# Half-array matmuls of a two-block transformer kernel rewritten for the whole 128x128 array

## Chip, cores and metric

The kernel runs on one core of a Trainium2 chip (trn2). The metric is device time in microseconds for one execution.

## What is computed

Two blocks of two layers each, in float32, on one sequence of 512 tokens of width 1024. A layer of the first block is a mixer (gated delta rule, top-k sparse attention and a gated linear recurrence side by side) and a feed-forward part; a layer of the second block is feed-forward, mixer (a linear recurrence, stick-breaking attention and forgetting attention), feed-forward. The parts that the change touches, cut to the core:

```python
# gated delta rule: 4 heads of 128, chunks of 64 tokens
T  = triangular_solve(eye + M, eye)                 # M strictly lower triangular, 64 x 64 for each chunk
u0 = T @ (beta * v);  wk = T @ (beta * exp(G) * k)
def step(state, ...):                               # 8 chunks, one after the other
    u = u0_c - w_c @ state
    o = qd_c @ state + qk_c @ u
    state = state * gl_c + kd_c.T @ u
# sparse attention, 4 heads of 64: an index score selects keys for each block of 128 queries
score = sum_h(relu(qi_h @ ki.T) * wi_h)
o = softmax(q_h @ k_sel.T / 8) @ v_sel
# second block, 4 heads of 64 each
z = q @ k.T / 8;  y_sb  = weights(z) @ v            # stick-breaking
y_fox = softmax(q @ k.T / 8 + Fq - Fk) @ v          # forgetting
```

## The kernel before

Activations lie transposed: features on the partitions, the 512 tokens along the free axis. Every large product (projections, feed-forward, output) is made in three passes of rounded operands: high part by high part, low by high, high by low (`hh,wh`, `hl,wh`, `hh,wl` in the profile; `wh` and `wl` are made from each loaded weight chunk `raw` by one ScalarE and one VectorE instruction). These are called dense here. Such a matmul is one record in the trace; the small products inside the mixers are plain float32 and leave two records each. All matmuls go through one helper line, L175 (transposes L181), all activations through L190, tensor-tensor operations of VectorE and GpSimd through L193, so that groups are told apart by the tile names.

The program is not issued in the order of its text. Each logical strand (a lane: `dn_prepare0`, `dn_scan1`, `dsa_choose`, `dsa0`, `hg1`, `fox0`, `sb0`, `weights`, `dense` ...) only records its steps with what they wait for. `interleave` then ranks the steps by their longest remaining path, plus hand-set leads for single lanes (`LEADS`, `WAYS`), and `schedule` writes a fixed instruction order for each engine by a cost model. On TensorE it knows the tile form of each matmul (`tile_of`: 128 or 64 rows, 128, 64 or 32 columns), counts a drain of the array when the form changes, keeps a model of the array's clock, prefers dense work when the clock would otherwise fall, and may put in empty matmuls (`nothing`, L259, `spinner,zeros`). Waits between engines stay semaphore waits.

The four mixers are the places where small products stand. `mixer1` runs twice, `mixer2` twice:

- `gates` turns the rows of wi, beta and the decay (4 transposes from partitions 64 to 127 of `tmp`).
- `dn_project`, `dn_prepare(p)` for two pairs of heads: the triangle of each 64-token chunk is inverted by doubling, in 5 rounds of 64x64 products (`bA`, `bB`, `bC`, `bMT`; two chunks at a time, one on partitions 0 to 63, one on 64 to 127). The solved triangle `Z` (`bB`) then multiplies `bV` (giving `u0`, tile `du`) and `bK` (giving `wk`, tile `dwk`), one 64-token chunk at a time.
- `dn_scan(r)`: eight steps for each pair; a step takes `wk` by the state (`ds,dwk`), subtracts it from `u0` into `u` (`du`), makes the new state from `kdec` and `u` (`du,dkd`), and the output from state by q (`dq,ds`) and `u` by `qk` (`dqk,du`).
- `dsa_choose`: index scores (`ki,qi`), then 16 rounds of max and match_replace on VectorE. `dsa_project` writes queries, keys and values over the same tiles `qi` and `ki`; `dsa_attend` runs 16 steps (4 query blocks, 4 heads), each with a score product (`ki,qi`), softmax, transposes, and the product with the values (`apt,av`), all through the one bank B[6].
- the gated linear recurrence (`hg_tile`): 64x64 products throughout (`hq,hk`, `ht`, `mod_sum`, `ha,hi`).
- `mixer2`: `sb_attention` (`sbq,sbk` scores, `sw,sbv` values), `fox_attention` (`fxk,fxq` scores, `fpt,fxv` values), `lru`. The values of two heads fill the two partition halves of one bank `bo`, which ScalarE copies out once for each pair of heads.

A head of 64 occupies 64 partitions, so the score products load 64 rows of the array, the value products write 64 columns, and the scan does either. The program's `project` hands out the dense projections, 28 tiles in `mixer1`, and the strands use up this dense work while they run.

## Time and profile before

| | |
|---|---|
| median of 3 runs | 3846.35 us (3844.14 to 3847.4) |
| profiled execution, its own time | 3846.75 us |
| its span | 3845.0 us |
| TensorE busy | 3753.6 us, 98% |
| VectorE, ScalarE, GpSimd busy | 2025.5, 1590.1, 184.1 us |
| mean granted TensorE clock | 0.961 |

The granted clock is given as a share of 2.4 GHz: 1.00 is that level and 0.50 is 1.2 GHz, and a value between is a stretch that had both. A busy TensorE is not TensorE at its peak: ends of matmuls are modelled in the record, so that a matmul that drains or that runs at half clock also counts as busy. How fast the array is fed is seen better in the times at which weight loads (PEld) start. "mean ns" of a matmul holds its latency, not only its share of the stream.

### The profile page before, as it was taken

How to read it: one execution, taken by the hardware profiler on the slowest of the kernel's cores; microseconds unless marked ns; L12 is line 12 of the kernel's file. 1: busy time of each engine (PE TensorE's matmuls, PEld its weight loads, DVE VectorE, ACT ScalarE, POOL GpSimd, SP SyncE). 2: the span in 40 equal slices, each digit the busy share in tenths (PEclk: the TensorE clock that was granted, in tenths of full speed). 3: DMA queues.
4: the chain of work that ended last, by engine and by line, in shares of the span. 5: the costliest groups of instructions: out<-in, count | busy, mean ns of one | idle time of the engine just before them, and what ended most of it. 6: DMA issues, size and time to landing. Idle time of an engine off the chain costs nothing.

```text
span 3845.0 us, 50935 instructions
## 1 busy us (share of the span) xinstructions
PE 3753.6 (98%) x21067; PEld 3062.8 (80%) x21067; DVE 2025.5 (53%) x3365; ACT 1590.1 (41%) x2465; POOL 184.1 (5%) x256
## 2 busy tenths in 40 slices
PE   9999999999999999999999998999999999989999
PEld 7877788887767688888888865988888888668888
DVE  6955377647764367745444465544443335554332
ACT  7445543326353343323222478322232225863221
POOL 1010100002010010001000010000000001000000
PEclk9978899999997799999999998999999999999999
DMA  3101134442111034443444311244422332112232
GB/s 118 62 28 34 55 116 145 146 143 81 56 45 34 1 110 148 145 153 109 148 148 149 104 50 44 92 150 147 151 98 98 96 96 69 50 39 89 98 98 89
DMA packets 108694, 368.27 MB, mean 96 GB/s; under 512 B 14128, under 2 KB 16560, under 8 KB 108464
## 3 DMA queue, kind: packets, MB, share of 16 engines
q1 hardware_dynamic: 108464, 365.02, 28.8%
q8 instruction: 167, 2.74, 0.3%
q14 instruction: 63, 0.52, 0.0%
HBM read 360.78 MB, written 4.19 MB: 95 GB/s over the span
## 4 chain that ended last, share of the span: by engine, by line
PE 78%; ACT 6%; DVE 4%; issue 2%; POOL 1%; POOLq 0%; ACTq 0%; DVEq 0%
PE bank L175 77%; ACT L398 2%; PE bank L259 1%; ACT tmp L190 1%; ACT wh L190 1%; DVE tmp L196 1%; PE bank L181 0%; DVE wl L193 0%; DVE score L217 0%; ACT lr L190 0%; DVE ast L214 0%; ACT hh L190 0%; POOL x L193 0%; ACT fl L190 0%; ACT lu L190 0%
## 5 line engine op out<-in xcount | busy, mean ns | idle before, releaser
L175 PE MATMUL bank<-hh,wh 128*128 128x512 f32 (+2 forms) x3424 | 1290.5, 377 | 15.8 <-ACT lg L190 10.4
L175 PE MATMUL bank<-hl,wh 128*128 128x512 f32 (+2 forms) x3424 | 1289.0, 376 | 0.0
L175 PE MATMUL bank<-hh,wl 128*128 128x512 f32 (+2 forms) x3424 | 1285.8, 376 | 0.1
L190 ACT ACTIVATE wh<-raw 128x1024 fp32r<-128x1024 f32 (+1 forms) x542 | 559.1, 1036 | 1464.2 <-PE bank L175 1457.5
L193 DVE TENSOR_TENSOR wl<-raw,wh 128x1024 fp32r<-128x1024 f32 (+1 forms) x542 | 652.5, 1207 | 809.9 <-ACT wh L190 809.4
L175 PEld LDWEIGHTS bank<-hh,wh 128*128 128x128 f32 (+1 forms) x3424 | 651.6, 190 | 144.4 <-issue 33.7
L175 PEld LDWEIGHTS bank<-hl,wh 128*128 128x128 f32 (+1 forms) x3424 | 651.6, 190 | 116.4 <-issue 12.3
L175 PEld LDWEIGHTS bank<-hh,wl 128*128 128x128 f32 (+1 forms) x3424 | 652.1, 190 | 115.6 <-issue 9.1
L175 PE MATMUL bank<-ah,wh 128*128 128x512 f32 (+1 forms) x1188 | 437.4, 368 | 0.0
L175 PE MATMUL bank<-ah,wl 128*128 128x512 f32 (+1 forms) x1188 | 436.9, 368 | 0.0
L175 PE MATMUL bank<-al,wh 128*128 128x512 f32 (+1 forms) x1188 | 436.5, 367 | 0.0
L175 PEld LDWEIGHTS bank<-ah,wh 128*128 128x128 f32 x1188 | 224.6, 189 | 35.8
L175 PEld LDWEIGHTS bank<-ah,wl 128*128 128x128 f32 x1188 | 224.6, 189 | 35.6
L175 PEld LDWEIGHTS bank<-al,wh 128*128 128x128 f32 x1188 | 224.6, 189 | 35.2
L398 ACT ACT_TABLE_LOAD x190 | 243.8, 1283 | 3.4
L196 DVE SCALAR_TENSOR_TENSOR mod_sum<-raw,cact,mod_sum 128x512 f32<-128x512 f32 x252 | 189.1, 750 | 29.3 <-DMA raw<-in_ada_dram 25.2
L193 DVE TENSOR_TENSOR gv<-bank,gv 128x512 f32<-128x512 f32 x88 | 60.9, 692 | 214.6 <-PE bank L175 213.0
L196 DVE SCALAR_TENSOR_TENSOR gv<-bank,small,gv 128x511 f32<-128x511 f32 (+1 forms) x176 | 130.9, 746 | 2.5
L190 ACT ACTIVATE ah<-gv 128x512 fp32r<-128x512 f32 x132 | 81.9, 620 | 104.0 <-DVE gv L193 104.0
L193 DVE TENSOR_TENSOR al<-gv,ah 128x512 fp32r<-128x512 f32 x132 | 90.7, 687 | 21.1 <-ACT ah L190 20.8
L196 DVE SCALAR_TENSOR_TENSOR x<-bank,dmod,x 128x512 f32<-128x512 f32 (+1 forms) x58 | 37.7, 658 | 120.3 <-PE bank L175 120.2
L193 POOL TENSOR_TENSOR x<-x,tmp 128x256 f32<-128x256 f32 x56 | 44.9, 827 | 855.7 <-DVE tmp L196 855.7
(367 smaller groups left out, 3772.3 us busy)
## 6 DMA issues: line engine op xcount, KB each, us to landing
raw<-in_up_dram SPq DMA_DIRECT2D x264, 512.0 KB, 3.3
raw<-in_ada_dram SPq DMA_DIRECT2D x144, 512.0 KB, 4.2
raw<-in_in_dram SPq DMA_DIRECT2D x88, 512.0 KB, 3.3
raw<-in_down_dram SPq DMA_DIRECT2D x96, 448.0 KB, 3.3
raw<-in_down_dram SPq DMA_DIRECT2D x48, 512.0 KB, 3.5
raw<-in_out_dram SPq DMA_DIRECT2D x32, 512.0 KB, 3.3
x<-in_x_dram SPq DMA_DIRECT2D x16, 256.0 KB, 5.0
raw<-in_in2v_dram SPq DMA_DIRECT2D x8, 512.0 KB, 3.7
```

Of the source, the lines that this page charges most:

```text
L175: s = self.put(lambda e: e.matmul(out, lhsT, rhs, **kw), records * max(records * n, 2 * m) / 2.4)
L190: return self.put(lambda e: e.activation(out, x, func, **kw), cost, tables)
L193: return self.vector(lambda e: e.tensor_tensor(out, a, b, op), width(out))
L196: return self.vector(lambda e: e.scalar_tensor_tensor(out, a, scalar, b, op0, op1), width(out), 125.0)
L259: s = Step(Queue(self, "nothing", "pe"), lambda e: e.matmul(out[:, 0:n], zeros, rhs, start=alone, stop=alone), [], n / 2.4)
L398: engine.preload_act_table_set(s.load)
```

## The change

Every product listed above that used half of the array's rows or columns is rewritten so that it addresses all 128 rows and 128 columns.

- Scan: `u` keeps zeros in the partitions of the other chunk (both `u` buffers of each pair are cleared once at the start of the mixer, and each buffer serves chunks of one half only). `kdec`, `qk` and `wk` are then taken over all 128 partitions or all 128 columns of the pair of chunks.
- Solved triangles: a new tile `bZ`, over the places of `bM` and `bMT`, is cleared by GpSimd after the last use of `bMT`; two ScalarE copies (64 partitions by 8x64) lay the two triangles of a pair of chunks on its diagonal. One matmul then serves both chunks, for `u0` and for `wk`. `bM` and `bMT` come free only after these products.
- Scores: `qi`, and in `mixer2` `sk` and `fq`, get a slot for each head, with zeros in the other head's partitions; so the copy out of PSUM is two instructions of 64 partitions in place of one of 128. The tiles are cleared by GpSimd at the start of the mixer.
- Values: the stationary operand is a 128-column pair of value blocks, the result is taken from the half that belongs to the head. In `mixer2` the bank `bo` is copied out once for each head (64 partitions by 512) and the next head's values wait for that.
- `gates` and `dsa_project` copy and transpose 128 rows in place of 64.
- `ysa`, `ysb` and `yfx` move into the slots of used queries or keys; the copies that write them wait for the score products that read them.

`LEADS` and `WAYS` stay as they are; the fixed order on each engine is worked out anew by `schedule`. The products of `hg_tile`, the five rounds of `dn_prepare` and its `chunks` and turn of `bM` keep their forms. The diff, cut to its core:

```diff
+    mem.bZ = mem.place("bZ", [P, 8, P], F32, b_at + 2048 * 3)
...
+    mem.av = mem.place("av", [P, 5, 64], F32, at)
+    at += 1024
...
-    mem.qi, mem.ki = put("qi", [P, 2, S]), put("ki", [P, S])
-    mem.av = put("av", [P, 4, 64])
+    mem.qi, mem.ki = put("qi", [P, 4, S]), put("ki", [P, S])
+    mem.ysa = mem.qi.rearrange("p (t x) s -> p t x s", x=2)[:, :, 0, :]
...
+    mem.padded = []
+    q = mem.lane("padding")
+    q.pool.wait_ge(before)
+    mem.padded.append(q.pool.memset(mem.qi[:, :, :], 0.0).then_inc(q.pool.sem, 1))
+    for v in mem.pairs:
+        for u in v.u.slots:
+            q.pool.wait_ge(before)
+            u.free = [q.pool.memset(u.ap[:, :, :], 0.0).then_inc(q.pool.sem, 1)]
...
-        rows = q.dve.tensor_copy(t.ap[64:128, :], b.ap[64:128, :]).then_inc(q.dve.sem, 1)
+        rows = q.dve.tensor_copy(t.ap[:, :], b.ap[:, :]).then_inc(q.dve.sem, 1)
         b.free = [k1, k2, rows]
         b = B[2]
-        for j in range(4):
-            q.pe.wait_ge(rows, b.free)
-            turned = q.pe.transpose(b.ap[:, 64 * j:64 * j + 64], t.ap[64:128, P * j:P * j + P], mem.k("ident")[64:128, 64:128]).then_inc(q.pe.sem, 1)
+        turned = transposes(mem, q, b, [t.ap[:, P * j:P * j + P] for j in range(4)], rows)
...
-        bMT.free, X.free, Y.free = [mx], [mx], [yz]
+        X.free, Y.free, apart = [mx], [yz], []
+        q.pool.wait_ge(mx, bM.free)
+        blank = q.pool.memset(mem.bZ[:, :, :], 0.0).then_inc(q.pool.sem, 1)
+        for h in range(2):
+            r0 = slice(64 * h, 64 * h + 64)
+            q.act.wait_ge(zs, blank)
+            apart.append(q.act.activation(mem.bZ[r0, :, 64 * h:64 * h + 64], Z.ap[r0, :, :], ACT.Copy).then_inc(q.act.sem, 1))
...
-                for h in range(2):
-                    r0 = slice(64 * h, 64 * h + 64)
-                    q.pe.wait_ge(zs, bv[e], b.free)
-                    m = q.pe.matmul(b.ap[r0, P * j:P * j + P], Z.ap[r0, 2 * j + e, :], bV.ap[r0, e, j, :], start=True, stop=True).then_inc(q.pe.sem, 1)
+                q.pe.wait_ge(apart, bv[e], b.free)
+                m = q.pe.matmul(b.ap[:, P * j:P * j + P], mem.bZ[:, 2 * j + e, :], bV.ap[:, e, j, :], start=True, stop=True).then_inc(q.pe.sem, 1)
...
-            b, m2 = prep.next(), None
-            for h in range(2):
-                r0 = slice(64 * h, 64 * h + 64)
-                other = m2
-                for j in range(4):
-                    at = P * j + 64 * h
-                    q.pe.wait_ge(zs, bk[e], other, b.free)
-                    m2 = q.pe.matmul(b.ap[:, at:at + 64], bK.ap[r0, e, j, :], Z.ap[r0, 2 * j + e, :], start=True, stop=True).then_inc(q.pe.sem, 1)
+            b = prep.next()
+            for j in range(4):
+                q.pe.wait_ge(apart, bk[e], b.free)
+                m2 = q.pe.matmul(b.ap[:, P * j:P * j + P], bK.ap[:, e, j, :], mem.bZ[:, 2 * j + e, :], start=True, stop=True).then_inc(q.pe.sem, 1)
...
-        bV.free, bK.free, Z.free = [m], [m2], [m2]
+        Z.free = apart
+        bM.free = bMT.free = [m, m2]
+        bV.free, bK.free = [m], [m2]
...
-                    m = q.pe.matmul(b.ap[r0, P * e:P * e + P], v.wk[:, e, at:at + 64], state.ap[:, e, :], start=True, stop=True).then_inc(q.pe.sem, 1)
+                    m = q.pe.matmul(b.ap[:, P * e:P * e + P], v.wk[:, e, P * j:P * j + P], state.ap[:, e, :], start=True, stop=True).then_inc(q.pe.sem, 1)
...
-                    m = q.pe.matmul(b.ap[:, P * e:P * e + P], v.kdec[r0, e, j, :], u.ap[r0, e, :], start=True, stop=True).then_inc(q.pe.sem, 1)
+                    m = q.pe.matmul(b.ap[:, P * e:P * e + P], v.kdec[:, e, j, :], u.ap[:, e, :], start=True, stop=True).then_inc(q.pe.sem, 1)
...
-                mo = q.pe.matmul(o, u.ap[r0, e, :], v.qk[r0, 2 * j + e, :], start=n == 0, stop=True).then_inc(q.pe.sem, 1)
+                mo = q.pe.matmul(o, u.ap[:, e, :], v.qk[:, 2 * j + e, :], start=n == 0, stop=True).then_inc(q.pe.sem, 1)
...
+    def heads(q, i, b, done, free, scale=None):
+
+        ready = []
+        for x in range(2):
+            rows = slice(64 * x, 64 * x + 64)
+            q.act.wait_ge(done, free)
+            ready.append(q.act.activation(mem.qi[rows, 2 * i + x, :], b.ap[rows, :], ACT.Copy, scale=scale).then_inc(q.act.sem, 1))
+        return ready
...
-                m = q.pe.matmul(b.ap[:, 0:n], mem.qi[lo:lo + 64, h // 2, P * i:P * i + P], mem.ki[lo:lo + 64, 0:n], start=True, stop=True).then_inc(q.pe.sem, 1)
+                b, t = dsa.next(), logit.next()
+                q.pe.wait_ge(qi_ready[h], gt["ki"], b.free)
+                m = q.pe.matmul(b.ap[:, 0:n], mem.qi[:, h, P * i:P * i + P], mem.ki[:, 0:n], start=True, stop=True).then_inc(q.pe.sem, 1)
...
+                at = 64 * ((k - h % 2) % 4)
                 q.pe.wait_ge(s, v_ready, b.free)
-                m = q.pe.matmul(b.ap[lo:lo + 64, 0:P], mem.av[:, k, :], pt.ap[:, P * k:P * k + P], start=k == 0, stop=k == i).then_inc(q.pe.sem, 1)
+                m = q.pe.matmul(b.ap[:, 0:P], pairs[:, at:at + P], pt.ap[:, P * k:P * k + P], start=k == 0, stop=k == i).then_inc(q.pe.sem, 1)
...
-            q.act.wait_ge(m)
+            q.act.wait_ge(m, multiplied[i, h], multiplied[i, h - h % 2])
...
-    mem.sq, mem.sk = put("sbq", [P, 2, S]), put("sbk", [P, 2, S])
+    mem.sq, mem.sk = put("sbq", [P, 2, S]), put("sbk", [P, 4, S])
...
+    for y in (mem.sk, mem.fq):
+        q.pool.wait_ge(before)
+        mem.padded.append(q.pool.memset(y[:, :, :], 0.0).then_inc(q.pool.sem, 1))
...
+            b, done = project(10 + i)
+            d[1, i] = []
+            for x in range(2):
+                rows = slice(64 * x, 64 * x + 64)
+                q.act.wait_ge(done, mem.padded)
+                d[1, i].append(q.act.activation(mem.sk[rows, 2 * i + x, :], b.ap[rows, :], ACT.Copy).then_inc(q.act.sem, 1))
+            b.free = d[1, i]
...
+                    for x in range(2):
+                        rows = slice(64 * x, 64 * x + 64)
+                        q.dve.wait_ge(r_ready, g8, mem.padded)
+                        d[n, i].append(q.dve.scalar_tensor_tensor(mem.fq[rows, 2 * i + x, :], b.ap[rows, :], mem.g8[rows, 0:1], r.ap[rows, :], ALU.mult, ALU.mult).then_inc(q.dve.sem, 1))
...
-            m = q.pe.matmul(b.ap[:, 0:n], mem.fq[lo:lo + 64, ti, P * i:P * i + P], mem.fk[lo:lo + 64, ti, 0:n], start=True, stop=True).then_inc(q.pe.sem, 1)
+            m = q.pe.matmul(b.ap[:, 0:n], mem.fq[:, h, P * i:P * i + P], mem.fk[:, ti, 0:n], start=True, stop=True).then_inc(q.pe.sem, 1)
+            multiplied.append(m)
...
-            if not (hp or i):
-                sums[:] = [bo.free]
             for k in range(i + 1):
-                q.pe.wait_ge(s, v_ready[k], sums)
-                m = q.pe.matmul(bo.ap[lo:lo + 64, P * i:P * i + P], mem.fv[:, k, 64 * h:64 * h + 64], pt.ap[:, P * k:P * k + P], start=k == 0, stop=k == i).then_inc(q.pe.sem, 1)
+                q.pe.wait_ge(s, v_ready[k], bo.free)
+                m = q.pe.matmul(bo.ap[:, P * i:P * i + P], mem.fv[:, k, P * ti:P * ti + P], pt.ap[:, P * k:P * k + P], start=k == 0, stop=k == i).then_inc(q.pe.sem, 1)
...
+            if i == 3:
                 q = mem.lane("fox0")
-                q.act.wait_ge(sums, columns, rows)
-                done.append(q.act.activation(mem.yfx[:, ti, :], bo.ap[:, :], ACT.Copy).then_inc(q.act.sem, 1))
+                q.act.wait_ge(sums, multiplied)
+                done.append(q.act.activation(mem.yfx[lo:lo + 64, ti, :], bo.ap[lo:lo + 64, :], ACT.Copy).then_inc(q.act.sem, 1))
...
-                    m = q.pe.matmul(z, mem.sk[lo:lo + 64, ti, P * i:P * i + P], mem.sq[lo:lo + 64, ti, P * i:S], start=True, stop=True).then_inc(q.pe.sem, 1)
+                    m = q.pe.matmul(z, mem.sk[:, h, P * i:P * i + P], mem.sq[:, ti, P * i:S], start=True, stop=True).then_inc(q.pe.sem, 1)
...
-                    q.pe.wait_ge(w_ready[i], v_ready[i], sums)
-                    m = q.pe.matmul(bo.ap[lo:lo + 64, P * i:S], mem.sv[:, i, 64 * h:64 * h + 64], w.ap[:, a0:a0 + n], start=i == 0, stop=i == 3).then_inc(q.pe.sem, 1)
+                    q.pe.wait_ge(w_ready[i], v_ready[i], bo.free)
+                    m = q.pe.matmul(bo.ap[:, P * i:S], mem.sv[:, i, P * ti:P * ti + P], w.ap[:, a0:a0 + n], start=i == 0, stop=i == 3).then_inc(q.pe.sem, 1)
...
-                sums.append(m)
-            q.act.wait_ge(sums, columns, rows)
-            done.append(q.act.activation(mem.ysb[:, ti, :], bo.ap[:, :], ACT.Copy).then_inc(q.act.sem, 1))
-            bo.free = [done[-1]]
-        return done
+                q.act.wait_ge(m, multiplied)
+                done.append(q.act.activation(mem.ysb[lo:lo + 64, ti, :], bo.ap[lo:lo + 64, :], ACT.Copy).then_inc(q.act.sem, 1))
```

## Rows read from the trace of the kernel before

**Rows 1.** The page: busy time and share of TensorE; granted clock in 40 slices.

```profile
PE 3753.6 (98%) x21067; PEld 3062.8 (80%) x21067; DVE 2025.5 (53%) x3365; ACT 1590.1 (41%) x2465; POOL 184.1 (5%) x256
...
PEclk9978899999997799999999998999999999999999
```

**Rows 2.** Windows of the four mixers: busy us of each engine, granted clock, DMA share, GB/s.

```profile
84.00:444.00 360.00, 345.58 (x2982) 270.71 (x2981) 227.73 (x473) 177.11 (x276) 39.31 (x44) 0.87 0.12 39
950.00:1340.00 390.00, 371.99 (x2957) 275.87 (x2955) 214.91 (x444) 164.53 (x264) 39.92 (x41) 0.84 0.11 35
2190.00:2406.00 216.00, 199.29 (x926) 139.16 (x925) 120.53 (x209) 164.02 (x263) 16.92 (x34) 0.94 0.15 49
3215.00:3440.00 225.00, 203.18 (x966) 141.46 (x965) 119.50 (x210) 165.56 (x267) 18.80 (x35) 0.96 0.15 49
```

**Rows 3.** Timeline of the weight loads over the four mixers: first row, last row.

```profile
84.00 0.41 PEld L259 LDWEIGHTS bank<-spinner,zeros 128*128 128x128 f32 x2
...
3439.88 0.19 PEld L175 LDWEIGHTS bank<-hh,wh 128*128 128x128 f32 x1
```

**Rows 4.** Timeline of weight loads: start, length, rows*columns of the array, count.

```profile
326.10 0.30 PEld L175 LDWEIGHTS bank<-dq,ds 128*128 128x128 f32 x2
326.31 0.19 PEld L175 LDWEIGHTS bank<-hh,wl 128*128 128x128 f32 x1
...
1221.78 0.19 PEld L175 LDWEIGHTS bank<-hl,wh 128*128 128x128 f32 x1
1222.01 0.19 PEld L175 LDWEIGHTS bank<-hh,wl 128*128 128x128 f32 x1
1222.55 0.19 PEld L175 LDWEIGHTS bank<-apt,av 128*64 128x64 f32 x2 [0.35 <-issue]
1222.91 0.19 PEld L175 LDWEIGHTS bank<-hh,wh 128*128 128x128 f32 x1 [0.17 <-issue]
```

**Rows 5.** The same timeline where the clock is at half.

```profile
295.65 0.50 PEld L175 LDWEIGHTS bank<-dq,ds 128*128 128x128 f32 x2
296.03 0.33 PEld L175 LDWEIGHTS bank<-hh,wl 128*128 128x128 f32 x1
...
1281.01 0.50 PEld L175 LDWEIGHTS bank<-dq,ds 128*128 128x128 f32 x2
1281.63 0.50 PEld L175 LDWEIGHTS bank<-dqk,du 64*128 64x128 f32 x2
```

**Rows 6.** The same timeline: solved triangle by bK, and by bV.

```profile
200.54 0.96 PEld L175 LDWEIGHTS bank<-bB,bK 64*128 64x128 f32 x8 [0.17 <-issue]
...
1012.90 0.85 PEld L175 LDWEIGHTS bank<-bV,bB 64*64 64x64 f32 x16 [0.17 <-issue]
```

**Rows 7.** The same timeline: two half-array products side by side.

```profile
1190.63 0.18 PEld L175 LDWEIGHTS bank<-bB,bK 64*128 64x128 f32 x1
1190.63 0.18 PEld L175 LDWEIGHTS bank<-dqk,du 64*128 64x128 f32 x1
```

**Rows 8.** Windows inside the mixers, columns as in rows 2.

```profile
252.00:300.00 48.00, 48.00 (x623) 41.16 (x623) 17.56 (x45) 7.77 (x20) 1.25 (x4) 0.50 0.01 1
312.00:372.00 60.00, 59.34 (x478) 45.16 (x476) 32.16 (x76) 40.80 (x67) 2.54 (x2) 1.00 0.11 36
1052.00:1124.00 72.00, 68.17 (x705) 52.10 (x705) 52.20 (x98) 44.24 (x71) 17.69 (x15) 1.00 0.14 45
1232.00:1310.00 78.00, 76.06 (x399) 51.18 (x400) 38.89 (x86) 34.27 (x67) 3.80 (x3) 0.56 0.06 21
372.00:408.00 36.00, 32.97 (x215) 22.28 (x216) 18.73 (x36) 19.13 (x36) 3.80 (x3) 0.72 0.09 30
2284.00:2368.00 84.00, 70.92 (x282) 47.18 (x281) 47.07 (x78) 81.40 (x110) 2.06 (x7) 0.93 0.14 45
```

**Rows 9.** Groups of instructions by form: ScalarE copy of a whole bank; GpSimd clearing.

```profile
L190 ACT ACTIVATE ysb<-bank 128x512 f32<-128x512 f32 x4 | 2.4, 594 | 7.3 <-PE bank L175 7.3
L223 POOL MEMSET wr<- 128x512 f32 x2 | 1.1, 528 | 1186.9 <-DVE x L196 1186.9
```

89 lines of the change are left out of this document (45 added, 44 removed).

## Prediction

> **What bounds the kernel now.** I read the page first. TensorE is busy for 98% of the span, and in its clock row only a few of the 40 slices stand below 9 tenths [rows 1]. They lie in the mixers, so the second view is the windows of the four mixers [rows 2], 1191 us in all. TensorE lacks 14.4, 18.0, 16.7 and 21.8 us of busy time there; VectorE and ScalarE have about half of the first two windows and ScalarE has 164 of 216 and 166 of 225 us in the last two. So `mixer1` is bound by TensorE's stream nearly throughout. `mixer2` is bound by it in its first third, and then by ScalarE, which has 81.4 of 84 us between 2284 and 2368 [rows 8]. Outside the mixers nothing that the change touches is issued.
>
> Busy says little about what TensorE does with its time, so the third view is the timeline of weight loads, from the first row to the last over the four windows [rows 3]. Merged, these windows hold 1037, 1034, 729 and 767 groups; I went through them for places where the tile form (rows*columns) changes: 244, 329, 99 and 94, together 766. What such a place costs is seen in single rows. Dense loads follow each other by 0.23 us (1221.78 to 1222.01); before a change of form the next load comes after 0.54. A small product of two records that keeps the form takes 0.21 (326.10 to 326.31), and one before a change takes 0.36 [rows 4]. So a change costs 0.31 us behind a dense matmul and 0.15 behind a small one. At half clock a small one takes 0.38 without and 0.62 with a change [rows 5], 0.24 more; behind a dense one I scale 0.31 to 0.42, an estimate.
>
> **The changed order of forms.** I took the order as it is and read the changed products as 128*128. Then 130, 225, 14 and 12 changes of form stay, and 385 go: 77 behind dense and 227 behind small ones at full clock, 75 behind small and 6 behind dense ones at half. 77 x 0.31 + 227 x 0.15 + 75 x 0.24 + 6 x 0.42 = 23.9 + 34.1 + 18.0 + 2.5 = 78.5 us, of which 22.2, 22.5, 17.6 and 16.2 lie in the four mixers. What stays in `mixer1` are mostly the 64x64 products of `hg_tile` and of the five rounds. The order will be written anew, so the count is an estimate: the scheduler can group less or more.
>
> How much lands in the time? In `mixer1` TensorE is idle for only 4% of the windows [rows 2], but its chains through VectorE and ScalarE run close behind; I take 70% of 44.7, 31 us (bounds 30% and all). In `mixer2` a faster TensorE meets ScalarE: I take 30% of 33.8, 10 us (bounds nothing and all).
>
> **Solved triangles.** The product with `bK` has eight loads in 0.96 us with the last at 0.19, 0.11 us each [rows 6]. Its 128 records become 64: 64 x 0.11 = 7 us, on the path 5. The product with `bV` has 16 loads in 0.85 us, 0.053 each [rows 6]: the two chunks already run side by side, and eight full ones at 0.11 take 0.88, so nothing is gained there. The Trainium skill, "TensorE: Matmul & The Clock Gate", section on packing small matmuls, says that tiles on different row groups run concurrently and that a short contraction alone takes as long as a full one. By it, padding never shortens a matmul and only gives concurrency away; the trace agrees for `bV` (0.053 against 0.11), and by it alone the sum would be just the loss that follows.
>
> The same concurrency happens by chance elsewhere: `bB,bK` and `dqk,du` start together at 1190.63 [rows 7]. I count 46 such starts in the four windows; full-array products can't do this, and each costs 0.11: 5 us, on the path 4.
>
> The remaining changed products keep their count, and what they load or stream keeps them at 0.11 a record (a value product with 64 columns, `apt,av`, takes the 0.36 of two records and a change, as above). More rows or columns cost nothing by these rows, except that a first load of 128 columns in place of 64 may show by half of 0.11; about 100 such starts would be 5 us at most, and I take 0.
>
> **Clock.** Two stretches are at reduced clock and made of small products of all kinds: 1232 to 1310 at 0.56, and 372 to 408 at 0.72. They pass 399 records in 78 us and 215 in 36 (5.1 and 6.0 a us), and the stretch from 312 to 372 at full clock passes 478 in 60, 8.0 a us [rows 8]. At that pace they would save 28 and 9 us, 37 in all; that is the upper bound, since dense work also stands in the fast stretch, and the lower bound is nothing. Before the clock fell, TensorE was fed with half-array products and changes of form, and both go away. I take 15. From 252 to 300 (0.50) the 64x64 products dominate and stay, so I expect no gain.
>
> The Trainium skill, same page, Part 1, says that the clock follows how busy TensorE is, and not how much of the array a matmul fills. By it the padding itself would leave the clock where it is; that is a rival below. The trace has TensorE at 76.06 busy of 78 with the clock at 0.56, so its busy row doesn't decide it.
>
> **What is added.** A ScalarE copy of a bank takes 0.59 us [rows 9], and half the partitions save nothing, as its time goes by the free axis. In each `mixer2` there are two more for `sk`, two for `ysb`, two for `yfx`: 6 x 0.59 = 3.5 us, 7 in both, in a time where ScalarE has no room; I take 5. The next head's values wait for the copy of `bo`, with nothing behind but other lanes' products, which the order puts between; 0 to 5 us a mixer, in the range. In each `mixer1`: four more copies for `qi` (2.4 us, under ScalarE's idle half), and for each pair two copies for `bZ` in the chain from the last `zs` to `u0`, 1.2 us a pair and 4.7 in all, if nothing else fills TensorE; I take 3. What waits behind them is `wk`, `u0` and the scan's first step. GpSimd clears `bZ` in 2 x 0.53 us [rows 9] while the last `yz` product and the subtraction behind it run; were it late, up to 1 us a pair. The clearing of `qi` (2.1 us), `u`, `sk` and `fq` (4.2 us) lies under the first three projections; GpSimd has 39 of 360 us of work there [rows 2]. `fq` has two more VectorE instructions, with VectorE at 120 of 216. No DMA is added. `bM` and `bMT` come free later: the second pair's first sums would have to wait for the first pair's products, which run at 200 [rows 6], before the stretch from 252 in which the second pair's rounds stand [rows 8]; nothing. Sum of the added: 8 us.
>
> **Sum.** -31 - 10 - 5 + 4 - 15 + 8 = -49 us on the profiled execution's 3846.75 (span 3845.0, 1.75 around it): 3798. The median of the runs is 0.4 lower; I leave it at 3798.
>
> **Rivals.**
> - The clock stays as it is (the page's rule): 3798 + 15 = 3813. For it: many dense-free stretches remain. Against it: with the changes of form gone the same products stand closer together.
> - Other engines take the place: ScalarE in `mixer2` gives nothing back, in `mixer1` only 30% of 44.7 lands (the scans go back and forth between TensorE and VectorE at each step), 13 + 2 for the triangles - 8 added = 7: 3840. For it: VectorE has 228 of 360 us and ScalarE 177 [rows 2]. Against it: TensorE's idle 4%.
> - All of it lands: 78.5 + 7 + 37 = 122: 3724. For it: in `mixer1` the order can even group better than I count. Against it: ScalarE in `mixer2`.
> - Slower: the dense stock runs out earlier. The projections are what keeps the clock up between the strands; with small products faster, the same leads spend them sooner, and 312 to 372 and 1052 to 1124, now at 1.00 [rows 8], fall to half. At 5.1 against 8.0 records a us such time grows by 0.56: 132 us give +74, on 3813: 3887. It decides from 34 / 0.56 = 60 us on. For it: from 252 to 300 exactly this already happened (0.50). Against it: the scheduler holds dense work back when its clock model falls.
>
> **How the numbers follow.** Chances: the forecast 0.40, clock unmoved 0.22, other engines 0.15, all of it 0.14, slower 0.09. The range has to leave out the slower case and little else: 3725 (the bound of all gains) to 3850 (past the third case, with its lost waits of `bo`). About 0.2% (7.7 us) is what a measurement of this kernel can tell from no change. Faster by more: 0.40 + 0.22 + 0.14 and half of the third case, 0.83; within: the other half, 0.08; slower: 0.09. The forecast's own range is 3780 to 3815.
>
> **What would show it.** In the timeline of weight loads the changes of form in the four mixers fall from 766 to about 380, in `mixer2` to under 20 each; `bB,bK` disappears with 64 records in its place; the windows of `mixer1` shrink by about 20 to 30 us each and those of `mixer2` by about 5; the clock of the second `mixer1` rises above 0.84. The prediction is wrong if the count falls and the windows stay (other engines), if new half-clock stretches stand where 1.00 was (dense stock), or if ScalarE's stretch in `mixer2` grows past its 7 us.

## The result, and the profile after

The changed kernel takes 3717.28 us (median of 4 runs, 3703.77 to 3719.11) against 3846.88 for the kernel before (3844.14 to 3848.83): ratio 0.9654 (0.9636 to 0.9673), 133 us of 3847 (126 to 140). I had forecast 3798, with a range from 3725 to 3850; the time lies 8 us below the range. The profiled execution took 3718.38 us, with a mean granted clock of 0.972 (before 0.961).

The page of the kernel after, the lines that answer to [rows 1]:

```profile
PE 3634.4 (98%) x20983; PEld 3055.5 (82%) x20983; DVE 2023.8 (54%) x3369; ACT 1607.3 (43%) x2496; POOL 203.4 (5%) x274
...
PEclk9979999999979999999999998999999999989999
```

The number of matmuls is nearly unchanged, and TensorE is busy for 119 us less. Since the order is made anew, the windows of [rows 2] no longer hold the same work. I therefore cut both traces at two landmarks, from the last `gv` write of the stage before a mixer to the first `gv` write of the feed-forward part behind it. The four stages take 513.4, 669.8, 434.6 and 436.0 us before and 467.8, 602.5, 422.8 and 430.4 after: -45.6, -67.4, -11.8 and -5.7. All else together changed by +1.9. Windows of these stages, before and then after (columns as in [rows 2]):

```profile
84.00:513.00 429.00, 412.24 (x3437) 333.97 (x3436) 262.68 (x551) 208.71 (x349) 52.07 (x60) 0.87 0.13 43
744.00:1414.00 670.00, 646.35 (x4483) 509.40 (x4482) 365.37 (x734) 285.47 (x484) 72.15 (x83) 0.90 0.20 65
2034.00:2468.00 434.00, 417.29 (x2207) 332.92 (x2207) 232.82 (x411) 235.22 (x385) 18.75 (x39) 0.97 0.25 80
3065.00:3501.00 436.00, 413.15 (x2189) 327.70 (x2188) 215.36 (x383) 236.80 (x384) 20.33 (x39) 0.98 0.20 64
sum 1969.00, PE 1889.03 PEld 1503.99 DVE 1076.22 ACT 966.20 POOL 163.31; mean PE 472.26 PEld 376.00 DVE 269.06 ACT 241.55 POOL 40.83
```

```profile
84.00:468.00 384.00, 370.73 (x3362) 318.03 (x3361) 257.17 (x544) 210.84 (x353) 52.13 (x58) 0.91 0.14 48
698.00:1301.00 603.00, 584.59 (x4459) 496.61 (x4458) 364.27 (x735) 298.03 (x499) 76.26 (x90) 0.94 0.22 73
1923.00:2345.00 422.00, 408.84 (x2224) 341.05 (x2224) 232.72 (x413) 234.59 (x388) 24.66 (x41) 0.97 0.25 82
2942.00:3373.00 431.00, 405.31 (x2195) 336.53 (x2194) 217.49 (x386) 238.98 (x388) 25.83 (x41) 0.97 0.20 65
sum 1840.00, PE 1769.47 PEld 1492.23 DVE 1071.65 ACT 982.43 POOL 178.89; mean PE 442.37 PEld 373.06 DVE 267.91 ACT 245.61 POOL 44.72
```

The reader is to see two things: the gain stands in TensorE's busy column (1889.0 to 1769.5, 119.6 of 129 us), and TensorE's idle rest is nearly the same (80.0 and 70.5 us). So nothing else became the bound. Two counts go with it, taken over whole stages from the timeline of weight loads and from the granted clock. Changes of form fell from 259, 353, 101 and 96 (809) to 114, 116, 14 and 16 (260). Time at half clock fell from 297 us to 194.

The added work, from the groups by form of the kernel after, answers to [rows 9]; the two lines of the solved triangles, from the timeline of weight loads, answer to [rows 6]:

```profile
L190 ACT ACTIVATE bZ<-bB 64x512 f32<-64x512 f32 x8 | 5.0, 630 | 11.4 <-DVE bB L193 11.3
L223 POOL MEMSET bZ<- 128x1024 f32 x4 | 3.8, 954 | 16.2 <-PE bank L175 16.2
L223 POOL MEMSET sbk<- 128x2048 f32 x2 | 3.6, 1811 | 0.0
L223 POOL MEMSET qi<- 128x2048 f32 x2 | 3.6, 1808 | 9.4 <-DMA x<-in_x_dram 9.3
```

```profile
183.93 1.06 PEld L175 LDWEIGHTS bank<-bZ,bK 128*128 128x128 f32 x8
184.91 0.97 PEld L175 LDWEIGHTS bank<-bV,bZ 128*128 128x128 f32 x8
```

The copies take 0.63 us (I had 0.59), the clearing 0.95 and 1.8 us (I had 1.06 and 2.1), and a full-array record about 0.12 us: eight of them, then the next group 0.98 later.

### The profile page after: what moved, and what is told of

It is laid out like the page before. It is cut to its first block, busy times and chain, and to the rows that moved or that the text cites. A ratio compares the mean times of both kernels' runs of the same rounds, so it can differ in the third digit from the quotient of the medians.

```text
span 3716.6 us, 50808 instructions
## 1 busy us (share of the span) xinstructions
PE 3634.4 (98%) x20983; PEld 3055.5 (82%) x20983; DVE 2023.8 (54%) x3369; ACT 1607.3 (43%) x2496; POOL 203.4 (5%) x274
## 4 chain that ended last, share of the span: by engine, by line
PE 86%; ACT 7%; DVE 6%; issue 1%; POOL 1%; DMA 0%; SPq 0%; DVEq 0%; ACTq 0%; POOLq 0%
PE bank L175 84%; ACT L398 3%; ACT tmp L190 1%; PE bank L259 1%; DVE wl L193 1%; PE bank L181 1%; DVE score L217 1%; ACT wh L190 1%; DVE ast L214 1%; ACT lr L190 0%; DVE tmp L196 0%; POOL x L193 0%; DVE dk L196 0%; DVE bA L193 0%; DVE dv L196 0%
## 5 line engine op out<-in xcount | busy, mean ns | idle before, releaser
L259 PE MATMUL bank<-spinner,zeros 128*128 128x512 f32 (+3 forms) x336 | 94.5, 409 | 0.0
```

The source lines that it names most:

```text
L259: s = Step(Queue(self, "nothing", "pe"), lambda e: e.matmul(out[:, 0:n], zeros, rhs, start=alone, stop=alone), [], n / 2.4)
```

## The experiments

All ratios are against the kernel before. The stage counts are those of the one profiled execution.

### Which part carries it

**`mixer2` as before, all else changed.** The layout, copies and half-array products of `mixer2` are put back:

```diff
-    mem.sq, mem.sk = put("sbq", [P, 2, S]), put("sbk", [P, 4, S])
+    mem.sq, mem.sk = put("sbq", [P, 2, S]), put("sbk", [P, 2, S])
...
-            m = q.pe.matmul(b.ap[:, 0:n], mem.fq[:, h, P * i:P * i + P], mem.fk[:, ti, 0:n], start=True, stop=True).then_inc(q.pe.sem, 1)
+            m = q.pe.matmul(b.ap[:, 0:n], mem.fq[lo:lo + 64, ti, P * i:P * i + P], mem.fk[lo:lo + 64, ti, 0:n], start=True, stop=True).then_inc(q.pe.sem, 1)
```

> The change in mixer1 alone; mixer2 is as before. Between landmarks the two mixer2 stages gave back 11.8 and 5.7 us of the 128.6. Theory A and C alike: 3717 + 17 = 3734 (3728 to 3740). If the stages interact through the order, more than 8 us away from that.

Measured: 3724.85 us, ratio 0.9677 (0.9652 to 0.9702), 9 us slower than the changed kernel by the ratios, where 17 were expected; the difference is at the edge of the interval. The two stages take 436.5 and 435.4 us with 102 and 95 changes of form: 18.7 us longer than in the changed kernel. The whole profiled execution is 14 us longer (span 3730.8 against 3716.6), so the rest of it is 4 us shorter.

**The scan alone on half the array.** Three lines are taken back:

```diff
-                    m = q.pe.matmul(b.ap[:, P * e:P * e + P], v.wk[:, e, P * j:P * j + P], state.ap[:, e, :], start=True, stop=True).then_inc(q.pe.sem, 1)
+                    m = q.pe.matmul(b.ap[r0, P * e:P * e + P], v.wk[:, e, at:at + 64], state.ap[:, e, :], start=True, stop=True).then_inc(q.pe.sem, 1)
...
-                mo = q.pe.matmul(o, u.ap[:, e, :], v.qk[:, 2 * j + e, :], start=n == 0, stop=True).then_inc(q.pe.sem, 1)
+                mo = q.pe.matmul(o, u.ap[r0, e, :], v.qk[r0, 2 * j + e, :], start=n == 0, stop=True).then_inc(q.pe.sem, 1)
```

> The changed kernel with the three products of the scan on half of the array again (352 of the records that changed in mixer1, in 3 of the 5 products of a scan step). Theory A: the scan makes most changes of form in mixer1, up to 4 for each of 32 steps; with two thirds of them back, 80 to 130 more changes, 20 to 35 us: 3737 to 3752. Theory C: the scan's rows matter for the clock between 300 and 350 and in the second layer; half-clock time up by 30 to 60 us and 15 to 40 us on the time, with few changes more. If the scan is hidden behind other work, 3717 to 3725.

Measured: 3778.91 us, ratio 0.9822 (0.9802 to 0.9842): 62 us slower than the changed kernel, with 260 more changes of form (225, 265, 14, 16). By its ratio, half of the gain hangs on the scan, and both count and time are far above what was expected (80 to 130 changes, 3737 to 3752). But the order was made anew here too: 34 of the 56 us by which the profiled execution is longer lie in the first stage, which takes 502.0 us.

### The array or the plan?

The forms of the products enter twice: on the chip, and in the cost model by which `schedule` writes the order. In the next two kernels the scheduler is told something else than what the chip does.

**Full array on the chip, planned as half.** In the changed kernel each changed product is given its old form for the planner only:

```diff
-    def matmul(self, out, lhsT, rhs, **kw):
+    def matmul(self, out, lhsT, rhs, form=None, **kw):
...
-        s.tile, s.records, s.size = tile_of(lhsT, out), records, n
+        s.tile, s.records, s.size = form or tile_of(lhsT, out), records, n
```

> The changed kernel, but the scheduler is told the old half-array forms of the changed products, so that the order is made as if nothing had been padded. Theory A (the gain is the array's: changes of form that are no longer there, both those of the old order and those that the new order can avoid): the changes of form in the four mixers come out near the 381 that the prediction counted for the old order, against 260 in the changed kernel, and at 0.2 to 0.25 us each the time is some 25 to 35 us above 3717: 3740 to 3760. Theory B (the gain is the new order's, whatever the array does): 3830 to 3850, near the kernel before. Theory C (the gain is mainly the clock, which the padded rows raise): the half-clock time in the mixers is as short as in the changed kernel (about 185 us in its four mixers, against about 280 before) and the time is 3720 to 3740 whatever the count of changes.

Measured: 3805.6 and 3805.5 us, ratio 0.9892 (0.9863 to 0.9921); two further executions took far longer (4600 us at a granted clock of 0.724, and 12442 us) and are left out, so this rests on two; why those took so long is open. This is a gain of 42 us; with the planner kept ignorant, the forecast of 49 would have come close. No theory fits: there are 428 changes of form, the time at half clock is as short as theory C wanted (184 us), and the time is 88 us above the changed kernel. Windows of its four stages:

```profile
84.00:504.00 420.00, 386.92 (x3374) 318.14 (x3373) 261.68 (x553) 210.26 (x356) 52.66 (x62) 0.93 0.13 44
734.00:1384.00 650.00, 609.06 (x4432) 500.20 (x4431) 365.71 (x735) 292.15 (x494) 74.78 (x90) 0.94 0.21 67
...
sum 1931.00, PE 1810.39 PEld 1491.29 DVE 1079.31 ACT 982.90 POOL 173.73; mean PE 452.60 PEld 372.82 DVE 269.83 ACT 245.73 POOL 43.43
```

TensorE's busy time falls by 79 us, but its idle time grows from 80 to 121. My reading, which no run tests, is that the order was laid out for slower products and the chains behind them don't keep up.

**Half array on the chip, planned as full.** The same the other way round, in the kernel before, with `form=((True, 128), (0, 0), 128, 128)` on each product that the change touches.

> The kernel before, but the scheduler is told that the changed products fill the whole array, so that it orders them as in the changed kernel, while the chip still gets half-array forms. Theory A: the real changes of form grow past the 766 of the kernel before, since nothing holds them back, and the time is 3850 to 3900. Theory B: much of the gain is there, 3740 to 3790. Theory C: the clock falls for longer than before, since the scheduler believes it high, 3860 or more.

Measured: 3797.44 us (3794.6 to 3802.3), ratio 0.9872 (0.9852 to 0.9893), with 813 changes of form on the chip; theory B had 3740 to 3790. The plan alone is worth 49 us while the array does what it did before, solved triangles included. Both kernels also shift thousands of instructions, so neither isolates the array; the next ones do.

### The array alone, in an unchanged order

These are the changed kernel with half-array operands put back but the full form told to the scheduler. The instruction order is then the same on every engine as in the changed kernel; only the extent of the operands differs. The solved triangles stay full.

```diff
+FULL = ((True, 128), (0, 0), 128, 128)
...
-                mo = q.pe.matmul(o, u.ap[:, e, :], v.qk[:, 2 * j + e, :], start=n == 0, stop=True).then_inc(q.pe.sem, 1)
+                mo = q.pe.matmul(o, u.ap[r0, e, :], v.qk[r0, 2 * j + e, :], form=FULL, start=n == 0, stop=True).then_inc(q.pe.sem, 1)
...
-                m = q.pe.matmul(b.ap[:, 0:P], pairs[:, at:at + P], pt.ap[:, P * k:P * k + P], start=k == 0, stop=k == i).then_inc(q.pe.sem, 1)
+                m = q.pe.matmul(b.ap[lo:lo + 64, 0:P], mem.av[:, k, :], pt.ap[:, P * k:P * k + P], form=FULL, start=k == 0, stop=k == i).then_inc(q.pe.sem, 1)
```

**Scan, scores and values half**, all of them:

> The changed kernel with every instruction in its place (the order on each engine is the same, and so are all copies and clearings), but the products of the scan, the scores and the values use half of the array again; the solved triangles stay full. In this order the forms then change about 780 times in the four mixers, against 260. Theory A (what the array saves is the changes of form, each at 0.15 to 0.31 us, all of it in the time since the order is the right one): 520 x 0.2 = 104 us more, 3800 to 3830. Theory A', half of them hidden by waits: 3765 to 3785. Theory C (the clock): half-clock time well above the 194 us of the changed kernel, 280 or more.

**Only those that fill half of the columns** (`ds,dwk` and all values):

> As the run before, but only the products that used half of the columns (wk by state, and the three value products) are half again; all rows stay full. The forms change about 486 times. Theory A: 226 more x 0.2 = 45 us, 3750 to 3770. Theory C, in the sense that full rows keep the clock up: half-clock time stays near 194 us.

**Only those that fill half of the rows** (`du,dkd`, `dqk,du`, all scores):

> As the run before, but only the products that used half of the rows (u by qk, kdec by u, and the three score products) are half again; all columns stay full. The forms change about 615 times. Theory A: 355 more x 0.2 = 71 us, 3775 to 3800, and the time for each added change is the same as with the columns. Theory C: the half-clock time rises clearly above that of the columns' run, and each added change costs more here than there.

| | us | ratio | changes of form | granted clock of its runs |
|---|---|---|---|---|
| changed kernel | 3717.28 | 0.9654 | 260 | 0.972 to 0.976 |
| columns half | 3734.79 | 0.9706 (0.9688 to 0.9724) | 484 | 0.973, 0.974 |
| rows half | 3757.90 | 0.9766 (0.9731 to 0.98) | 615 | 0.971 to 0.978 |
| all half | 3779.23 | 0.9821 (0.9772 to 0.9869) | 778 | 0.969 to 0.980 |

By the ratios the array is worth 64 us here (0.0167 x 3847; the intervals leave about 20 either way), and 20 for the columns and 43 for the rows add up to it. With 518 changes of form between, each lands with 0.12 us in the time. The two parts came out below their expectations (3750 to 3770 and 3775 to 3800), which had 0.2 us a change: it is 0.09 for the 224 of the columns and 0.12 for the 355 of the rows, and the intervals are too wide to tell these two apart. The same stretch of the first mixer, all half and then changed (timeline of weight loads; start, length, rows*columns):

```profile
333.82 0.19 PEld L175 LDWEIGHTS bank<-hl,wh 128*128 128x128 f32 x1
334.37 0.29 PEld L175 LDWEIGHTS bank<-dqk,du 64*128 64x128 f32 x2 [0.36 <-issue]
334.73 0.19 PEld L175 LDWEIGHTS bank<-hh,wl 128*128 128x128 f32 x1
334.84 0.42 PEld L175 LDWEIGHTS bank<-dq,ds 128*128 128x128 f32 x2
335.18 0.19 PEld L175 LDWEIGHTS bank<-hh,wh 128*128 128x128 f32 x1
335.62 0.29 PEld L175 LDWEIGHTS bank<-dqk,du 64*128 64x128 f32 x2 [0.25 <-issue]
335.98 0.55 PEld L175 LDWEIGHTS bank<-ht 64*64 64x64 f32 x16
336.59 0.19 PEld L175 LDWEIGHTS bank<-hl,wh 128*128 128x128 f32 x1
337.02 0.19 PEld L175 LDWEIGHTS bank<-ds,dwk 128*64 128x64 f32 x2 [0.24 <-issue]
```

```profile
332.90 0.19 PEld L175 LDWEIGHTS bank<-hl,wh 128*128 128x128 f32 x1
333.13 0.42 PEld L175 LDWEIGHTS bank<-dqk,du 128*128 128x128 f32 x2
333.47 0.19 PEld L175 LDWEIGHTS bank<-hh,wl 128*128 128x128 f32 x1
333.58 0.42 PEld L175 LDWEIGHTS bank<-dq,ds 128*128 128x128 f32 x2
333.92 0.19 PEld L175 LDWEIGHTS bank<-hh,wh 128*128 128x128 f32 x1
334.03 0.42 PEld L175 LDWEIGHTS bank<-dqk,du 128*128 128x128 f32 x2
334.52 0.54 PEld L175 LDWEIGHTS bank<-ht 64*64 64x64 f32 x16
335.13 0.19 PEld L175 LDWEIGHTS bank<-hl,wh 128*128 128x128 f32 x1
335.24 0.42 PEld L175 LDWEIGHTS bank<-ds,dwk 128*128 128x128 f32 x2
```

Row by row it is the same work. Behind the dense load `dqk,du` starts after 0.55 us with the half form and after 0.23 with the full one: 0.32, the 0.31 that I had read before the change. The stretch takes 3.20 us with half products and 2.34 with full ones. The longer load of `dqk,du` (0.42 for 0.29) doesn't delay what follows. Over both runs of `mixer1` the groups of weight loads show the same in their idle column, again all half and then changed:

```profile
L175 PEld LDWEIGHTS bank<-dqk,du 64*128 64x128 f32 x128 | 19.5, 192 | 8.1 <-issue 5.4
L175 PEld LDWEIGHTS bank<-du,dkd 64*128 64x128 f32 x112 | 16.0, 190 | 8.3 <-issue 6.7
```

```profile
L175 PEld LDWEIGHTS bank<-dqk,du 128*128 128x128 f32 x128 | 22.2, 207 | 1.4
L175 PEld LDWEIGHTS bank<-du,dkd 128*128 128x128 f32 x112 | 18.4, 204 | 4.2 <-DVE du L193 0.9 <-issue 0.5
```

The granted clock decides the other question. In the same order the executions of the half-array kernel were granted 0.969 to 0.980, on both sides of the changed kernel's 0.972 to 0.976. Its profiled execution had 137 us at half clock where the changed kernel's had 194. Filling less of the array doesn't lower the clock here. Whether it raises it stays open. In the profiled executions of these four kernels the five rounds of the second pair ran at full clock with all half and rows half, and mostly at half clock in the changed kernel and with the columns half; but they ran at half clock in the kernel before too, which has half rows. The window of all half, to be held against the last one of this document:

```profile
236.00:280.00 44.00, 42.23 (x719) 33.68 (x720) 27.80 (x63) 17.91 (x36) 6.85 (x9) 1.00 0.05 14
```

That is one execution of each kernel, and other executions of all half had a mean clock 0.011 lower.

### Is the other half luck of the order?

**The kernel before, and the kernel after, with a shaken order.** One latency of the planner's table is changed by 10 ns:

```diff
-        ("dve", "pe"): 203.0, ("dve", "pool"): 155.0, ("pe", "act"): 197.0, ("pe", "dve"): 196.0,
+        ("dve", "pe"): 203.0, ("dve", "pool"): 155.0, ("pe", "act"): 207.0, ("pe", "dve"): 196.0,
```

> The kernel before with one number of the scheduler changed by 10 ns (the time from TensorE to ScalarE, 197 to 207), so that the same products are issued in another, equally reasoned order. It says how much the order alone can move the time by luck. If the gain of 130 us has a large part of chance (theory L: the order before happens to be a poor one), this moves by 20 us or more towards the changed kernel: 3825 or less. If the order before is ordinary, 3835 to 3865.

> The changed kernel with the same number changed by 10 ns. If its order is a lucky one, 3735 or more; if ordinary, 3705 to 3730.

Measured: before 3840.49 us, ratio 0.9981 (0.9969 to 0.9994); after 3713.61, 0.9648 (0.9626 to 0.967). Shaking moves either kernel by 2 to 7 us, with at most 16 changes of form more or less in a stage. Luck of that size doesn't explain the other 69 us of the 133. It is one shake of each kernel, though, and further down single edits tip the first stage by about 30 us; that such a tip is part of the 69 is not excluded. Before and all half, same order, differ by 38 us in the first stage (513.4 and 475.2) and by 51 in the second (669.8 and 619.1).

### Which figure of the planner?

The planner uses the form in two ways. It decides where the array has to drain (matmuls under way must end before the form changes), which products may overlap and which one keeps the form; and it adds up the array's activity in its own model of the clock, where a product of 64 rows counts half (line 130). When that model falls behind its goal, dense work or an empty matmul is put in.

**The kernel before, rows counted in full.** One line of the planner; every product on the chip stays as it was:

```diff
-                w.add(at, end, s.records * s.size * rows / 128)
+                w.add(at, end, s.records * s.size * 128 / 128)
```

> The kernel before, all forms as they are, but the scheduler's model of the clock counts every matmul as if it filled all 128 rows (drains are still modelled). The run with half forms and the changed kernel's order kept its granted clock at 0.969 to 0.980, as high as with full forms, so on the chip the rows do not seem to matter, and the model of the kernel before may hold the array for colder than it is. Theory P (the padding helps since it makes the scheduler's clock model right): 3800 to 3820, clock 0.97. Theory D (the scheduler's view of drains, not of the clock, is what made the old order slow): 3840 to 3855.

Measured: 3785.44 us (3777 to 3790), ratio 0.983 (0.9806 to 0.9853), mean granted clock 0.973 to 0.977; this is faster than the 3800 to 3820 of theory P. The same work on the same half-array products is 65 us faster by a changed order alone, in which the planner also puts more empty matmuls (225 records of L259 for 173 in these two stages). Windows of its first two mixer stages:

```profile
84.00:490.00 406.00, 394.38 (x3468) 322.14 (x3467) 261.23 (x552) 208.89 (x351) 51.96 (x60) 0.93 0.14 45
730.00:1360.00 630.00, 607.99 (x4508) 494.92 (x4507) 365.85 (x737) 294.12 (x491) 72.05 (x83) 0.94 0.22 71
```

The granted clock is that of the changed kernel's windows or above (0.93 and 0.94, before 0.87 and 0.90). The counts that go with it: in the second stage TensorE goes between dense and small work 308 times in place of 356, the changes of form in the two stages fall from 612 to 508, and their time at half clock from 253 us to 139. When three quarters of the small records of that stage were loaded (empty matmuls left out), 71% of its dense loads had been used; before it was 75%. A planner that undercounts the half products believes its clock to be in danger, puts dense work between them and has less of it left for the last quarter. The counts are measured; that they are what makes the time is argued. The other traces bear on it. In the second stage all kernels fall into two kinds: 75% in the kernel before, its shaken twin, full planned as half and the scan half (670, 667, 649 and 625 us), 71% in all others (588 to 644 us). In the first stage there is no such rule: the two longest shares, 67%, go with 551 and 504 us in the two kernels that follow, but 63% goes with anything from 467 to 522.

**The kernel before, drains not planned, rows still counted half.**

```diff
-                mo = q.pe.matmul(o, u.ap[r0, e, :], v.qk[r0, 2 * j + e, :], start=n == 0, stop=True).then_inc(q.pe.sem, 1)
+                mo = q.pe.matmul(o, u.ap[r0, e, :], v.qk[r0, 2 * j + e, :], form=((True, 128), (0, 0), 64, 128), start=n == 0, stop=True).then_inc(q.pe.sem, 1)
```

> The kernel before, forms on the chip as they are, but the scheduler takes the products that the change touches as being of the full form (no drain planned), while its clock model still counts half rows for them. With both planned full the time was 3797. Theory D: 3795 to 3810, nearly all of it. Theory P: 3835 to 3850, nothing of it.

Measured: 3862.69 us, ratio 1.0032 (1.0016 to 1.0049), 12 us slower than the kernel before by the ratio. Leaving the drains out of the plan gains nothing. Half on the chip, planned as full, differs from this kernel in one figure only, the rows counted for the products that the change touches, and is faster by 0.016, or 62 us. So the activity count is the figure that matters. Of it, 47 us are in the first stage (551.1 and 503.8).

**The changed kernel, the same products counted half in the activity** (`form=((True, 128), (0, 0), 64, 128)` on what had been half of the rows):

> The changed kernel with full forms on the chip and no drain planned, but the scheduler's clock model counts half rows for the products that had half rows before. Theory P: it loses what the kernel before gained by the opposite edit, 3717 + 50 to 70 = 3767 to 3787, with the half-clock time up from about 190 to 280 us. If the order's gain comes from somewhere else: 3710 to 3735.

Measured: 3744.62 us, ratio 0.973 (0.9714 to 0.9746), 29 us slower than the changed kernel; less than the 65 the other way round. Its time at half clock is 168 us, not more than the changed kernel's 194. The first stage is 36 us longer (504.1) and has 66 more changes of form, the second 12 shorter. Its executions were granted 0.977 to 0.979, more than the changed kernel's. The direction holds, the mechanism by way of the clock doesn't hold for this kernel.

**The changed kernel, all rows counted in full** (the line of the diff above, which now acts on the products that stayed half: `hg_tile` and the five rounds):

> The changed kernel, but the scheduler's clock model counts the 64x64 products that are left (recurrence and doubling rounds) as full rows too. Theory P (the model of the kernel before held the array for colder than it is, whatever the product): a further gain, smaller than the 65 us of the kernel before since only one kind of product is left, 3690 to 3710. If the model was wrong only for the padded products, no change or a loss: 3710 to 3730.

Measured: **3697.25 us** (3685.4 to 3701.6), ratio 0.9605 (0.9584 to 0.9626). This beats both kernels, by 20 us and 150 us. It has 139 us at half clock, the changed kernel 194, and its executions were granted 0.977 to 0.982.

**The changed kernel, form kept three times as readily.**

```diff
-                return (r[0] - way["slack"][behind] * (dense == behind) - way["stay"] * (s.tile[0] == array.mode)
+                return (r[0] - way["slack"][behind] * (dense == behind) - 3 * way["stay"] * (s.tile[0] == array.mode)
```

> The changed kernel, with the scheduler's preference for staying in a form (stay) three times as large. The products are the same; only the order differs. If the 230 changes of form that are left in mixer1 are still on the path, fewer of them (say 180) give 10 us: 3700 to 3712. If the order has other things to win or lose, the time moves by up to 20 us either way with no relation to the count of changes.

Measured: 3727.41 us (3701.5 to 3752.4), ratio 0.9686 (0.9635 to 0.9738); changes of form 104, 112, 14 and 12. No gain can be told from it, and the 3700 to 3712 of the first expectation is not reached.

### Two parts of `mixer1`

**Sparse attention on half the array**, and **solved triangles chunk by chunk**, each planned as it is:

```diff
-                m = q.pe.matmul(b.ap[:, 0:n], mem.qi[:, h, P * i:P * i + P], mem.ki[:, 0:n], start=True, stop=True).then_inc(q.pe.sem, 1)
+                m = q.pe.matmul(b.ap[:, 0:n], mem.qi[lo:lo + 64, h, P * i:P * i + P], mem.ki[lo:lo + 64, 0:n], start=True, stop=True).then_inc(q.pe.sem, 1)
```

```diff
-                m = q.pe.matmul(b.ap[:, P * j:P * j + P], mem.bZ[:, 2 * j + e, :], bV.ap[:, e, j, :], start=True, stop=True).then_inc(q.pe.sem, 1)
+                for h in range(2):
+                    r0 = slice(64 * h, 64 * h + 64)
+                    q.pe.wait_ge(apart, bv[e], b.free)
+                    m = q.pe.matmul(b.ap[r0, P * j:P * j + P], mem.bZ[r0, 2 * j + e, 64 * h:64 * h + 64], bV.ap[r0, e, j, :], start=True, stop=True).then_inc(q.pe.sem, 1)
```

> The changed kernel with the scores and values of the sparse attention on half of the array again, scheduler told so. The same edit to the scan cost 62 us with 260 changes of form more. There are 272 such records in mixer1 against the scan's 352; in proportion 35 to 50 us: 3750 to 3767. If it is only the scan that matters: under 3735.

> The changed kernel with the solved triangles multiplied one chunk at a time again (the copies to the diagonal tile stay). The prediction put this part at 7 us, 5 of them in the time; they are few stretches, so few changes of form: 3717 + 5 to 12 = 3722 to 3729.

Measured: 3723.63 us (3700.4 to 3763.5), ratio 0.9658 (0.9605 to 0.9712, the longest execution left out), and 3741.83, ratio 0.9737 (0.971 to 0.9765). Neither is as priced. The sparse attention has 147 more changes of form in `mixer1`, and its median is within its spread of the changed kernel's. But that spread is the clock's: 3700 and 3705 us had 0.987 and 0.985, and the execution at 0.975 took 3742, where the changed kernel takes 3716 at 0.974. So at the same clock it may well cost some 25 us; one execution can't show it. The triangles cost 25 us by the medians and 32 by the ratios, far above their 7. Both come with a new order, and the first stage has two kinds of length over all kernels here: 456 to 475 us (the changed kernel and its shaken twin, those in its order, `mixer2` as before, all rows counted in the changed kernel, form kept three times as readily, sparse attention half) and 490 to 551 (all those built on the kernel before, full planned as half, the scan half, the triangles half with 495.0, rows counted half with 504.1). The profiled execution with half triangles is 21 us longer than the changed kernel's, and its first stage 27. The place of the second pair's rounds doesn't tell the kinds apart: they start at 250 with a stage of 467 us and at 235 with one of 504. What tips the planner from one kind into the other I did not find.

## Why the prediction was wrong

**The step that failed is "I took the order as it is and read the changed products as 128*128".** I kept the effect on the array and left out that the same change alters a figure by which the order is written. The two together:

- The array, in an unchanged order: 64 us, give or take 20 (all half, same order). The forecast's term of 41 us for 385 changes was about the right size: at the measured 0.12 us each, 385 would be 48. The full price read in single rows was confirmed in place (0.32 for 0.31), and about 60% of the priced 0.20 a change lands; I had taken 70% and 30%.
- The order: the remaining 69 us of 133, which also hold the full triangles and the added copies and clearing. That the count of rows in the planner is enough for such an effect is shown by the 65 us that it gives to the kernel before with no product changed, and by the 62 us between the two kernels that are planned without drains and differ in that count alone. That it makes up all of the 69 is not shown; the reverse test gave 29.

By the other terms:

- **Changes of form.** 766 to about 381 was forecast, with 130 and 225 in `mixer1`. In the new order 114 and 116 stay, and 14 and 16 in `mixer2`, where I had 14 and 12. In `mixer2`, where the order could shift little, the count was right to within four; in `mixer1` the planner grouped much better. I had named this ("the scheduler can group less or more") and put no price on it.
- **What lands in `mixer2`.** Forecast 10, less 5 for ScalarE; measured 17.5 together (11.8 + 5.7). ScalarE gives back more than I allowed: the bounds had it, the 30% were too low.
- **Solved triangles.** The rows are nearly as forecast (0.12 us a record for 0.11, 64 records each). What the part is worth could not be separated from the order (25 to 32 us with a new one).
- **Lost overlap.** Half-row products can run side by side by chance; I charged 4 us for losing this. It is far outweighed: the kernel that keeps half rows, and with them the overlap, is 43 us slower. The loss by itself was not measured.
- **Clock.** I took 15 us for "half-array products and changes of form" going away. The clock did rise, from 0.961 to 0.972, but not for that reason: with half products in the same order it is as high (0.969 to 0.980), and with the planner's line alone it reaches 0.973 to 0.977. At the 3 us for each 0.001 of the last section the rise goes with some 33 us of the 133, an estimate, and by these two runs it belongs to the order. The Trainium skill, "TensorE: Matmul & The Clock Gate", Part 1, has the clock follow how busy TensorE has been. It doesn't speak of how much of the array is filled; that this has no part in it was my reading, and the runs here show no fall of the clock with half-filled products. My rival that rested on it was right that the padding doesn't lift the clock, wrong that the clock stays, and its 3813 wrong about the time.
- **Added work.** The durations held within 0.1 us each for the copies. Nothing in the stage windows shows it as a cost: ScalarE's sum grew by 16 us over the four stages and TensorE's idle time didn't.
- **Rivals.** "All of it lands" (3724, chance 0.14) is 7 us from the result, by luck: it has 37 us of clock from the padding and the full price of all 385 changes, where 64 us in all is the array's. "Slower" by a dense stock that runs out has its mirror image here: in the second mixer the stock lasts longer (71% used at three quarters of the small records, before 75%). That the planner no longer spends it on products that it undercounted is my reading; in the first mixer the shares hardly differ (61% and 63%). The half-clock stretch of the five rounds, 252 to 300 before [rows 8], now lies from 236 to 280, and stayed at 0.50 as I expected. My reason, that the 64x64 products dominate there, doesn't hold: all half has the same rounds in the same order in this window at 1.00.

```profile
236.00:280.00 44.00, 44.00 (x631) 40.34 (x628) 18.88 (x48) 9.48 (x18) 2.19 (x5) 0.50 0.05 14
```

What stays open: what in the order makes the two kinds of first stage; how much of the 69 us, and of what the triangles cost, is that; why the activity count is worth 65 us in one kernel and 29 in the other; and what gives one and the same kernel a higher or lower clock.

## What to carry to other kernels

Where small products stand between dense ones, a half-array form costs the change of form on either side. Padding with zeros to the whole array took that away here, and by more than the lost chance to run half tiles side by side. If a program plans its order by a cost model, a change to the products is also a change to the model: price it twice, and test the two apart by telling the planner one thing and the chip another. And a figure of such a model that doesn't match the chip (here, rows counted into the activity) can be worth as much as the array's part of the change, 65 us beside 64; look for it first, it is one line.

## What the runs showed of the hardware

Executions of one and the same kernel differ in their mean granted clock, and the time goes with it. All half, same order: 3761 us at 0.980 and 3796 at 0.969. Form kept three times as readily: 3701 at 0.982, 3752 at 0.966. Sparse attention half: 3700 at 0.987, 3763 at 0.965. That is about 3 us for each 0.001, nearly the whole spread of these kernels, so differences under 10 us need several runs each, and a single profile of such a kernel should be read beside its clock.
